# Scaled chunks and squares of the residual steps in PSUM instead of SBUF, and two-chunk groups drained one chunk at a time, in a three-block float32 network

## What is computed

```
h = [meta, x]
layer 0: h += 0.5*swiglu(rms(h));  h += rwkv7(rms(h));  h += 0.5*swiglu(rms(h))
layer 1: h += 0.5*swiglu(rms(h));  h += sparse_attention(rms(h));  h += 0.5*swiglu(rms(h))
h = h[16:]
block 2: h += W_o [dilated_attention | latent_attention](rms(h));  h += W_ff2 relu(W_ff1 rms(h))^2
rms(h) = h / sqrt(mean(h*h) + eps) * g ;  swiglu(x) = (silu(x W_gate) * (x W_up)) W_down
```

## Time and profile before

| | us |
|---|---|
| median of 3 runs | 1781.03 |
| lowest, highest | 1777.22, 1782.37 |
| profiled execution, own time | 1785.45 |
| its span | 1783.4 |

### The profile page before, as it was taken

The page is one execution under the profiler, slowest core; times in us unless marked ns, Lnnn a source line. Parts: engine busy times, 40 slices in busy tenths (PEclk is TensorE's granted clock), DMA queues, the critical chain, the costliest instruction groups (busy, mean ns, idle before and its releaser), DMA issues.

```text
span 1783.4 us, 40019 instructions
## 1 busy us (share of the span) xinstructions
PE 1612.4 (90%) x15940; PEld 1522.0 (85%) x15940; DVE 801.8 (45%) x1576; ACT 739.8 (41%) x1204; POOL 1097.2 (62%) x552
## 2 busy tenths in 40 slices
PE   6999979659888899999999997999989969869998
PEld 6999979438886799999999985699989957769998
DVE  4332374684435733343334477663345635453300
ACT  4444434512312344444444432644435434544532
POOL 5778857343301578787787763068868753328896
PEclk9999989768767899999999997999999988889999
DMA  6454533100010344455444542035436632214552
GB/s 228 165 180 147 195 115 138 43 1 2 3 49 25 119 159 171 144 186 189 166 172 150 198 144 95 1 129 186 172 126 203 185 126 95 95 48 165 188 192 91
DMA packets 38777, 231.27 MB, mean 130 GB/s; under 512 B 4511, under 2 KB 7680, under 8 KB 17552
## 3 DMA queue, kind: packets, MB, share of 16 engines
q1 hardware_dynamic: 34560, 225.49, 35.9%
q10 hardware_dynamic: 4112, 4.31, 1.1%
HBM read 227.09 MB, written 2.62 MB: 129 GB/s over the span
## 4 chain that ended last, share of the span: by engine, by line
PE 77%; DVE 11%; issue 7%; POOL 3%; ACT 1%; DMA 0%; SPq 0%; DVEq 0%; ACTq 0%; POOLq 0%
PE PS L737 62%; POOL wlo L691 3%; PE PS L736 1%; DVE xl L1618 1%; DVE xg L1702 1%; DVE ss L1632 1%; PE PS L915 1%; PE PS L930 1%; PE PS L954 1%; PE PS L922 1%; DVE score L2038 1%; PE PS L960 1%; PE PS L1284 1%; ACT whi L2395 1%; DVE prnb L2316 1%
## 5 line engine op out<-in xcount | busy, mean ns | idle before, releaser
L691 POOL TENSOR_TENSOR wlo<-raw,whi 128x1024 fp32r<-128x1024 f32 (+1 forms) x472 | 1036.1, 2217 | 579.7 <-ACT whi L2395 530.2
L737 PE MATMUL PS<-xh,whi 128*128 128x272 f32 (+1 forms) x2336 | 689.5, 295 | 79.1 <-POOL wlo L691 35.9
L737 PE MATMUL PS<-xl,whi 128*128 128x272 f32 (+1 forms) x2336 | 678.5, 290 | 0.0
L737 PE MATMUL PS<-xh,wlo 128*128 128x272 f32 (+1 forms) x2336 | 677.3, 290 | 0.0
L2395 ACT ACTIVATE whi<-raw 128x1024 fp32r<-128x1024 f32 (+1 forms) x472 | 447.5, 980 | 260.0 <-PE PS L737 205.9
L737 PEld LDWEIGHTS PS<-xh,whi 128*128 128x128 f32 x2336 | 451.1, 193 | 93.4 <-issue 35.9
L737 PEld LDWEIGHTS PS<-xl,whi 128*128 128x128 f32 x2336 | 452.7, 194 | 0.6
L737 PEld LDWEIGHTS PS<-xh,wlo 128*128 128x128 f32 x2336 | 452.4, 194 | 0.0
L737 PE MATMUL PS<-hid_h,whi 128*128 128x272 f32 (+1 forms) x960 | 274.9, 286 | 12.1 <-POOL wlo L691 11.9
L737 PE MATMUL PS<-hid_h,wlo 128*128 128x272 f32 (+1 forms) x960 | 274.4, 286 | 0.0
L737 PE MATMUL PS<-hid_l,whi 128*128 128x272 f32 (+1 forms) x960 | 273.6, 285 | 0.0
(11 more groups left out here) (382 smaller groups left out, 1771.8 us busy)
## 6 DMA issues: line engine op xcount, KB each, us to landing
raw<-w_f_in_in SPq DMA_DIRECT2D x88, 1024.0 KB, 4.8
raw<-w_f_dn_in SPq DMA_DIRECT2D x64, 704.0 KB, 4.0
raw<-w_b_ff_in SPq DMA_DIRECT2D x32, 1024.0 KB, 4.8
raw<-w_rk_r_in SPq DMA_DIRECT2D x4, 1024.0 KB, 4.8
raw<-w_rk_k_in SPq DMA_DIRECT2D x4, 1024.0 KB, 4.7
raw<-w_rk_v_in SPq DMA_DIRECT2D x4, 1024.0 KB, 4.8
raw<-w_rk_o_in SPq DMA_DIRECT2D x4, 1024.0 KB, 4.9
raw<-w_at_q_in SPq DMA_DIRECT2D x4, 1024.0 KB, 5.0
```

Source lines behind the costliest of these rows:

```text
L691: nc.gpsimd.tensor_tensor(wlo[U % SPL][:, part], raw[U % RAW][:, part], whi[U % SPL][:, part].bitcast(F32), ALU.subtract).then_inc(s_lo, 1)
L737: mm(out, a, b, start=start and n == 0, stop=stop and n == 2, **kw)
```

## The change

The tiles `xg` and `sq` leave SBUF. `xg(m, n)` is now bank 4 + m % 2 of PSUM and `sq(m, n)` bank 6 + m % 2: one chunk to a bank, two chunks deep. The residual step goes by single chunks everywhere: in a group of two, the first chunk is added as soon as its own half of the unit is done (for b_o as soon as the group is), the second raises `group_drained`. `xl` now comes ahead of the sum of squares, and ScalarE copies to `xh` ahead of squaring. With only two buffers, VectorE waits for `x_low` of the chunk before last, and ScalarE for its sum. Since bank 4 is now in use at the end of f3_dn, the matmul for the bias table moves behind the first unit of b_cq.

```diff
-NORMS = [("f0", 8), ("rk", 8), ("f1", 4), ("f2", 8), ("at", 8), ("f3", 4), ("b", 8), ("ff", 4)]
+NORMS = [(_name, 8) for _name in ("f0", "rk", "f1", "f2", "at", "f3", "b", "ff")]
-        sq = ff("sq", [128, 2, 2, T])
-        xg = ff("xg", [128, 2, 2, T])
+        def xg(m, n):
+            return PS[:, 4 + m % 2, 0:n]
+        def sq(m, n):
+            return PS[:, 6 + m % 2, 0:n]
...
-            pe.wait_ge(s_bc, 112)
-            mm(PS[0:8, 4, 0:384], relb[:, :], distt[:, :], start=True, stop=True).then_inc(s_bwm, 1)
...
             for u in range(3):
                 b_pairs("b_cq", u, norm="b" if u == 0 else None)
+                if u == 0:
+                    pe.wait_ge(s_bc, 112)
+                    mm(PS[0:8, 4, 0:384], relb[:, :], distt[:, :], start=True, stop=True).then_inc(s_bwm, 1)
...
-                groups, per = 8 // w, 4 if w == 2 else 2
-                def add(j, i):
+                per = 8 if w == 2 else 2
+                def add(m, i):
+                    j, q = m // w, m % w
                     U, G = U0[name] + units * (j + 1) - 1, G0[name] + j
-                    src = PS[:, bank(G):bank(G) + w, 0:n]
+                    src = PS[:, bank(G) + q, 0:n]
...
+                    elif w == 2:
+                        dve.wait_ge(s_unit, 2 * U + q + 1)
...
+                    ins = v.scalar_tensor_tensor(x, src, factor, x, ALU.mult, ALU.add)
+                    if q == w - 1:
+                        ins.then_inc(s_free, 1)
+                    else:
+                        step.do(ins)
...
+                    if m >= 2:
+                        dve.wait_ge(s_x, val(X0[split] + m - 1, i, per))
+                    v.tensor_scalar(xg(m, n), x, gm, None, ALU.mult).then_inc(s_xm, 1)
+                def after_act(m, i):
+                    if g is not None:
+                        dve.wait_ge(s_xh, val(X0[split] + m + 1, i, per))
...
+                        low(xl[0][:, o, 0:n].rearrange("p o n -> p (o n)"), xg(m, n),
+                            xh[0][:, o, 0:n].rearrange("p o n -> p (o n)"), s_x)
+                    dve.wait_ge(s_sq, val(Q0[norm] + m + 1, i, per))
+                    add_squares(norm, m, sq(m, n), n, i)
...
-                    f(sq[:, j % 2, 0:w, 0:n], x, ACT.Square).then_inc(s_sq, 1)
-                    for q in range(w if split else 0):
-                        m = j * w + q
...
+                    for m in range(j * w, j * w + w):
...
+                        if split:
+                            act.wait_ge(s_xm, val(XM0[split] + m + 1, i, per))
...
+                            f(xh[0][:, o, 0:n].rearrange("p o n -> p (o n)"), xg(m, n), ACT.Copy).then_inc(s_xh, 1)
+                        else:
+                            act.wait_ge(s_free, val(G0[name] + j + 1, i, per))
+                        if m >= 2:
+                            act.wait_ge(s_ssa, val(8 * N0[norm] + m - 1, i, per))
+                        f(sq(m, n), x, ACT.Square).then_inc(s_sq, 1)
```

More of the change, by code:

```diff
@@ L1677, in residual, with chunk @@
             def residual(name, n, w, units, factor, norm, g, split, last=False):
-                groups, per = 8 // w, 4 if w == 2 else 2
-                def add(j, i):
+                per = 8 if w == 2 else 2
+                def chunk(m, i):
+                    return hv(n, m)[:, 0, :] if i is None else h[:, bass.ds(i * per + m, 1), T - n:T].rearrange("p o n -> p (o n)")
+                def add(m, i):
+                    j, q = m // w, m % w
                     U, G = U0[name] + units * (j + 1) - 1, G0[name] + j
-                    src = PS[:, bank(G):bank(G) + w, 0:n]
+                    src = PS[:, bank(G) + q, 0:n]
@@ L1685, in add @@
                     if last:
[L1686 removed]
+                        src = PS[:, j, q * n:q * n + n]
                         dve.wait_ge(*((s_unit, 2 * (U0[name] + 3 + j // 2)) if j % 2 else (b_om, j // 2 + 1)))
+                    elif w == 2:
+                        dve.wait_ge(s_unit, 2 * U + q + 1)
                     else:
                         dve.wait_ge(s_unit, val(2 * (U + 1), i, 2 * per * units))
[L1690 to L1693 removed]
@@ L1694, in add @@
-                    v.scalar_tensor_tensor(x, src, factor, x,
-                                           ALU.mult, ALU.add).then_inc(s_free, 1)
+                    x = chunk(m, i)
+                    ins = v.scalar_tensor_tensor(x, src, factor, x, ALU.mult, ALU.add)
+                    if q == w - 1:
+                        ins.then_inc(s_free, 1)
+                    else:
+                        step.do(ins)
                     if g is None:
                         return
-                    dve.wait_ge(s_free, val(G + 1, i, per))
@@ L1699, in add @@
-                    for q in range(w):
-                        m = j * w + q
[L1701 to L1714, removed]
+                    if q == w - 1:
+                        dve.wait_ge(s_free, val(G + 1, i, per))
+                    else:
+                        step.sync()
@@ L1715, in after_act @@
+                    if m >= 2:
+                        dve.wait_ge(s_x, val(X0[split] + m - 1, i, per))
+                    gm = col(g + m) if i is None else vec[:, bass.ds(i * per + (g + m), 1)]
+                    v.tensor_scalar(xg(m, n), x, gm, None, ALU.mult).then_inc(s_xm, 1)
+                def after_act(m, i):
+                    if g is not None:
                         dve.wait_ge(s_xh, val(X0[split] + m + 1, i, per))
                         o = slice(m, m + 1) if i is None else bass.ds(i * per + m, 1)
-                        low(xl[0][:, o, 0:n].rearrange("p o n -> p (o n)"), xg[:, j % 2, q, 0:n],
+                        low(xl[0][:, o, 0:n].rearrange("p o n -> p (o n)"), xg(m, n),
@@ L1718, in after_act, with body @@
                             xh[0][:, o, 0:n].rearrange("p o n -> p (o n)"), s_x)
[L1720 to L1724, removed]
+                    dve.wait_ge(s_sq, val(Q0[norm] + m + 1, i, per))
+                    add_squares(norm, m, sq(m, n), n, i)
+                def body(ms, i):
+                    for m in ms:
+                        add(m, i)
+                        if m >= 1:
+                            after_act(m - 1, i)
@@ L1725, in residual @@
                 start_sum()
-                turns(step, groups, per, 0, body, 1)
-                after_act(groups - 1, None)
+                turns(step, 8, per, 0, body, 1)
+                after_act(7, None)
             def split_input(name, b, made, n, chunks=range(KC), at0=0):
```

22 lines of the change are left out of this document (9 added, 13 removed).

## The result

The changed kernel took 1759.67 us, median of four runs (1750.15 to 1766.12), against 1781.57 us for the kernel before on the same chip. The ratio is 0.9872, with an interval of 0.9836 to 0.9909. The profiled execution took 1762.79 us, with a span of 1761.0 and a mean granted clock of 0.931.

The account below looks back on a forecast made before the run. It took the kernel as a long run of TensorE matmuls with only the holes to win; 7.1 + 3.0 + 2.0 + 1.7 + 0.3 - 1.3 = 12.8 us off 1781.0 gave 1768.2 us, range 1761.5 to 1776.5.

Parts of the forecast that it names:

- Part 3: b_o to b_ff1: TensorE starts 1.2 us later but then runs without a hole; gain 2.0 us (0.5 to 3.5).
- Part 4: The kernel's start: the fourth chunk's slow `xl` loses some 2.05 us; gain 1.7 us (1.2 to 2.4).
- the four large parts: Part 1, Part 2, Part 3 and Part 4, all forecast as gains: 7.1, 3.0, 2.0 and 1.7 us.
- Part 1: rk_o to f1: chunk-by-chunk draining keeps up with TensorE, as after f1_dn; gain 7.1 us (6.0 to 7.4).
- Part 2: at_o to f3: ScalarE's `whi` starts 2.4 us earlier, so unit 2 comes earlier; gain 3.0 us (2.2 to 4.4).
- Part 5: f1_dn, f2_dn, f3_dn: earlier `xl` saves, ScalarE's later square costs; together +0.3 us (-0.5 to +1.0).
- Part 6: Bias table: the moved bias matmul delays the issue of the write to memory; -1.3 us (-2.5 to +0.3).
- A: Loops: gain multiply, input in SBUF, still stands behind GpSimd despite its PSUM output; time 1773.3, chance 0.12.
- B: Residual steps: ScalarE's PSUM writes or two-buffer waits stretch a chunk from 1.6 to 2.3 us; time 1775.1, chance 0.13.
- C: Behind the seams: steady stretches begin earlier but weights are missing, holes reappear one unit on; time 1779, chance 0.08.
- D: Bias table: the write, issued later and sharing DMA engines, lands 19 to 21 us later; time near 1787, chance 0.04.

Follow-up runs that it names:

- the last experiment: The changed kernel with one ScalarE rounding of 1 us done twice, right behind the wait for the bias write; median 1766.13 us, ratio 0.9909.

## Why the prediction was right or wrong

The step that failed is the clock behind the holes. The sum took the clock as a discount on two gains (2.0 in Part 3, 1.7 in Part 4) and put the stages that the change does not touch at nothing, without a reason. Measured in the profiled pair, Part 3 was 4.4 and Part 4 3.7, and the last block's attention won 5.5 more by its granted clock. Which instructions speed up, and which waits go, was right, and so were the signs of the four large parts. The seams alone would have given 18.5 us, a time just inside the range; the attention's 5.5 against the scan's -2.7 did most to take it out.

**Part 1 (7.1).** Measured 7.8 up to f1's first instruction, 8.1 a little further; the upper bound was 7.4. The comparison of the two seams was the right way to price it. One part of the reason falls: "with GpSimd no longer in its way" is worth only 0.9 us here. The single draining does the rest, even with all buffers in SBUF, since it brings VectorE's last work into GpSimd's pause. Taking PSUM alone, with pairs, gives 4.3.

**Part 2 (3.0).** Between the end of the sparse attention and f3's steady part I measured 2.8 us in the first profile and 2.9 in the second. TensorE has no waits for `xl` left at this seam; it waits 2.38 us for `wlo` instead, and ScalarE's `whi` starts 2.3 us earlier (2.4 forecast). That the sum came so near is in part luck: the terms shown from 1183.05 on (2.0, 4, 1.0 and 2.5) give 1192.6 and a gain of 3.3, not 1192.9; with the 2.0 as part of the 4, as it reads, they give 1190.6 and 5.3. The sparse attention ahead of it won 0.3 and 3.2 us, which the forecast did not have.

**Part 3 (2.0).** This is the term that failed most, 4.4 us against bounds of 0.5 and 3.5. The mechanism held: TensorE starts later, at 11.4 us after the first add (11 forecast), and then runs on. Here are its rows after the change, beside the earlier trace rows:

```profile
1567.86 0.58 PE L741 MATMUL PS<-xh,whi 128*128 128x256 f32 x1 [9.42 <-DVE h L1701]
1572.83 0.59 PE L751 MATMUL PS<-ss,ones 128*128 128x256 f32 x2
1584.37 0.38 PE L741 MATMUL PS<-xh,whi 128*128 128x256 f32 x1 [2.40 <-POOL wlo L695]
```

norm_sum stands 16.4 us after the first add, before it was 18.7: 2.3 won, where the forecast had 2.4. The wrong step was the next: "since the clock must recover anyway and had half recovered, I take 2.0". An unbroken run got its clock back sooner, so 0.7 more was won up to rms, and after the gap ahead of unit 2 the clock stayed at 1.00, where before it fell. The two windows before:

```profile
1602.40:1606.40 4.00, 1.65 (x10) 0.82 0.00 0
1606.40:1610.40 4.00, 4.00 (x28) 0.75 0.24 51
```

and after:

```profile
1580.40:1584.40 4.00, 1.60 (x15) 1.00 0.00 0
1584.40:1588.40 4.00, 4.00 (x34) 1.00 0.08 16
```

That is another 1.35 us. I had counted the clock as a discount on the gain, and here it is a premium. It is not a sure one: five executions with this draining of b_o in PSUM won 4.35 to 4.5 us, the one with the bias matmul early 3.9, and of the two kernels with b_o alone in pairs one had the last 1.35 us and the other did not. The 3.47 us hole of the earlier trace rows was GpSimd's doing, for it is not quiet at this seam either. VectorE in time, before, beside a subtraction of GpSimd's from 1586.43 on:

```profile
1586.20 2.93 DVE L1632 TENSOR_TENSOR ss<-ss,sq 128x256 f32<-128x256 f32 x2
1589.17 2.78 DVE L1618 TENSOR_TENSOR xl<-xg,xh 128x256 fp32r<-128x256 f32 x2
```

**Part 4 (1.7).** Measured 3.7 (and 3.2 to 4.6 in the nine other profiles with the same start), against bounds of 1.2 and 2.4. The 2.05 us of the slow `xl` were right, and the steady stretch starts 2.6 us earlier. The rest is that TensorE reaches its full pace earlier: 19 matmuls in 2 us already from 20 us on, while before there were still 10 from 22 to 24. The stretch of 1032 matmuls took 129.30 us instead of 130.35. Again "as the matmuls here are the slow ones of a start, not all of it reaches the stretch" had the sign wrong. The experiments show the scaled chunk's place as the cause: with it in SBUF the start won 0.4 us, with the squares there too it lost 1.0.

**Part 5 (+0.3)** came to -0.2, inside its bounds but with the other sign: 0.3 at f1_dn and f2_dn, -0.5 at f3_dn. **Part 6 (-1.3)** came to -0.2: the write to memory moved with the rest (13.10 us behind the last add of f3_dn, before 13.03), and undoing the edit won 0.3 us.

**What the sum left out** is the largest item: 5.5 us in the last block's attention, which I had not looked at because no line of it changes. By the last experiment it hangs on timing to the microsecond, through the granted clock. No row of before would have given its sign, but busy windows at 0.50 and 0.66 were there to see, and they say that some us can move either way. The range was too narrow by that. Against it stood the scan, -2.7 in the profiled pair.

**The rivals.** A falls: the gain multiply with its input in SBUF and its output in PSUM takes 504 ns beside GpSimd. B falls: a chunk at b_o takes 1.63 us (1.6 forecast), and ScalarE's writes to PSUM take 0.38 us. C falls: f1 runs 1032 matmuls in 129.30 us from 608.61 on. D falls: the wait is 18.06 us. Its price, a write that lands 19 to 21 us later, was worked out from no row, and no run tested it.

The Trainium skill's rule that a single-source float32 instruction loses its double rate with a PSUM operand (VectorE: DVE Perf Modes, "Why PSUM operands drop a tier") is borne out by this case: the gain multiply takes 0.50 us with a PSUM output and 0.36 with an SBUF one, the 0.14 us of its estimate. Where GpSimd works it is paid back: 1586 ns with an SBUF output, 504 with a PSUM one. Its other rule (SBUF — State Buffer, the section on the two separate sides) has the multiply held up for its two-port mode, and the sums and `xl` for their two SBUF inputs. All placements here agree: each of the three came to about 0.5 us or less with a single operand in PSUM. By that rule rival A should have had less than its 0.12, since the multiply gives up the mode for which it would wait.

## What to carry to other kernels

When two engines shut each other out of SBUF, first look where the pauses of the blocking engine are: finer draining that moves the exposed work into a pause can win as much as another placement, and which of the two wins differs from seam to seam, so each seam wants its own choice (pairs at b_o, single chunks at rk_o). Price a seam with the clock that follows it, and give that term a wide range: in most executions unbroken runs of TensorE won nearly twice what the removed waits themselves came to (4.4 for 2.3 at b_o, 3.7 for 2.05 at the start), in some less (3.9 and 3.2). And list the long waits that no one disputes; the largest gain of this study, 13.5 us, came from moving one wait for a DMA behind four units of work that did not need it.

## What the runs showed of the hardware

- TensorE's granted clock made the same instructions of an attention stage take 5.5 us less or 3.8 us more than in the kernel before, with shifts of about a microsecond between the kernels. One added instruction of 1.0 us cost 6.9. Yet with the kernel unchanged from its bias table to b_o, six profiled executions agree there to 0.3 us, piece by piece; a seventh, with both buffers in SBUF, does not (2.6 us won for 5.5). The Trainium skill (TensorE: Matmul & The Clock Gate, "What's actually happening") says that the clock's reckoning is free-running and does not start with the kernel; the scan, which differs by 7.0 us between two executions of the kernel before, looks like that, the last attention, as repeatable as it is, does not.
- In the RWKV scan, the same 155 or so matmuls took 4.4 us at a granted clock of 1.00 in one execution of a kernel and 8.0 at 0.50 in another. Over two executions of the kernel before the scan differs by 7.0 us, over all kernels by 10.5. Elsewhere these two agreed to 0.2 us; the two of the changed kernel differ at the start (0.7), the RWKV inputs (1.0), the scan (0.7) and the sparse attention (2.8), and by 0.2 or less at every other place. So at the seams, comparisons by stage tell 0.5 us apart, where medians of six runs don't tell 5.
- In the first 24 us the records of the kernel before show a granted clock of 1.00, yet 9 or 10 matmuls run in 2 us where 19 do later. At a kernel's start, the pace has to be read from the matmuls themselves:

```profile
20.00:22.00 2.00, 2.00 (x9) 1.00 0.11 45
```

(the kernel before), against the changed kernel's

```profile
20.00:22.00 2.00, 2.00 (x19) 1.00 0.01 4
```
